# Position mix of a gated MLP block: both parts of the mixing weights in one 256-column matmul, and the later channel groups between the k tiles of the output projection

## The reference

```python
z = jax.nn.gelu(h @ w_in)
u, v = jnp.split(z, 2, axis=-1)
v = rmsnorm(v, v_g)
v = v.reshape(bsz, n, A_CHUNK, A_GROUPS, A_GDIM)           # chunks of 128 rows, 8 groups of 128 channels
ws = jnp.where(causal[None], w_s, jnp.zeros_like(w_s))      # 8 matrices of 128 x 128
s = jnp.einsum('gts,bnsgc->bntgc', ws, v) + b_s.T[None, None, :, :, None]
return (u * s.reshape(bsz, L, A_WIDTH)) @ w_out
```

## Time and profile before

| | |
|---|---|
| median of 3 runs | 1896.01 us (1891.55 to 1899.03) |
| the profiled execution's own time | 1891.51 us |
| its span, first to last instruction | 1889.7 us |
| TensorE busy | 1830.5 us, 97% of the span |
| VectorE busy | 1063.4 us, 56% |
| ScalarE busy | 769.9 us, 41% |
| GpSimd busy | 399.7 us, 21% |
| mean granted TensorE clock | 0.988 of full speed |

### The profile page before, as it was taken

The page is one execution under the profiler, slowest core; times in us unless marked ns, Lnnn a source line. Parts: engine busy times, 40 slices in busy tenths (PEclk is TensorE's granted clock), DMA queues, the critical chain, the costliest instruction groups (busy, mean ns, idle before and its releaser), DMA issues.

```text
span 1889.7 us, 20269 instructions
## 1 busy us (share of the span) xinstructions
PE 1830.5 (97%) x8329; PEld 1522.0 (81%) x8329; DVE 1063.4 (56%) x1025; ACT 769.9 (41%) x850; POOL 399.7 (21%) x386
## 2 busy tenths in 40 slices
PE   7999999999999999999979999998999999999997
PEld 5888888888888787888768888876888888888885
DVE  4463365265255665555575455657766666866664
ACT  5533543533433633344443434353333335333331
POOL 4442440450331033311112211132000002000001
PEclk9999999999999999999989999998999999999998
DMA  8545754753753778876957776799644545845542
GB/s 293 209 166 193 256 207 150 277 209 129 294 201 136 276 270 277 307 248 216 370 181 256 273 251 223 255 368 387 271 187 183 214 182 188 301 179 188 213 178 89
DMA packets 130268, 437.02 MB, mean 231 GB/s; under 512 B 7272, under 2 KB 8320, under 8 KB 115072
## 3 DMA queue, kind: packets, MB, share of 16 engines
q1 hardware_dynamic: 105920, 338.71, 50.0%
q0 software_dynamic: 23056, 88.61, 12.7%
q10 hardware_dynamic: 1200, 8.40, 1.1%
HBM read 309.87 MB, written 125.83 MB: 231 GB/s over the span
## 4 chain that ended last, share of the span: by engine, by line
PE 90%; DVE 3%; DMA 3%; ACT 1%; issue 1%; SPq 0%; DVEq 0%; POOL 0%; ACTq 0%
PE bank L1078 59%; PE bank L943 28%; PE bank L980 2%; DMA u_raw<-in_mlp_w 2%; PE bank L967 1%; DMA a_raw<-a2s 1%; DMA Y<-x1s 0%; DVE Y L894 0%; DVE sums L880 0%; DVE sums L887 0%; DVE r L877 0%; DVE u_lo L727 0%; DMA xin<-in_x 0%; DVE sums L885 0%; DVE sums L883 0%
## 5 line engine op out<-in xcount | busy, mean ns | idle before, releaser
L1078 PE MATMUL bank<-x_hi,u_hi 128*128 128x512 f32 x896 | 352.5, 393 | 21.5 <-DVE c L869 14.2
L1078 PE MATMUL bank<-d_hi,a_hi 128*128 128x512 f32 x896 | 350.0, 391 | 10.4 <-DVE Y L869 8.6
L1078 PE MATMUL bank<-x_lo,u_hi 128*128 128x512 f32 x896 | 351.0, 392 | 0.0
L1078 PE MATMUL bank<-x_hi,u_lo 128*128 128x512 f32 x896 | 350.8, 392 | 0.0
L1078 PE MATMUL bank<-d_lo,a_hi 128*128 128x512 f32 x896 | 349.6, 390 | 0.0
L1078 PE MATMUL bank<-d_hi,a_lo 128*128 128x512 f32 x896 | 349.5, 390 | 0.0
L727 DVE TENSOR_TENSOR u_lo<-u_raw,u_hi 128x1024 fp32r<-128x1024 f32 x112 | 144.4, 1290 | 232.8 <-ACT u_hi L516 232.7
L869 DVE TENSOR_TENSOR Y<-bank,Y 128x512 f32<-128x512 f32 x224 | 147.9, 687 | 196.0 <-PE bank L1078 191.4
L521 ACT ACTIVATE d_hi<-d_raw 128x2048 fp32r<-128x2048 f32 x56 | 107.4, 1918 | 318.0 <-DMA d_raw<-w2sum 188.2
L721 DVE TENSOR_TENSOR w_lo<-w_raw,w_hi 128x2048 fp32r<-128x2048 f32 x48 | 121.2, 2532 | 195.2 <-ACT w_hi L511 194.7
L1078 PEld LDWEIGHTS bank<-x_hi,u_hi 128*128 128x128 f32 x896 | 169.9, 190 | 59.3 <-issue 18.2
(11 more groups left out here) (105 smaller groups left out, 2819.0 us busy)
## 6 DMA issues: line engine op xcount, KB each, us to landing
a2s<-sums SPq DMA_DIRECT2D x32, 1792.0 KB, 12.6
a_raw<-a2s SPq DMA_DIRECT2D x56, 1024.0 KB, 7.1
w_raw<-in_a_w_in SPq DMA_DIRECT2D x32, 1024.0 KB, 6.5
job<-in_mlp_w POOLq DMA_DIRECT2D x32, 1024.0 KB, 6.8
u_raw<-w1sum SPq DMA_DIRECT2D x64, 512.0 KB, 4.2
d_raw<-w2sum SPq DMA_DIRECT2D x32, 1024.0 KB, 4.9
u_raw<-in_mlp_w SPq DMA_DIRECT2D x48, 512.0 KB, 5.6
d_raw<-in_mlp_w SPq DMA_DIRECT2D x24, 1024.0 KB, 5.1
```

Of the source, the lines that this page charges most:

```text
L1078: ins = pe.matmul(bank_of(g, j)[:, :], stationary[x_part][:, k, j * P:(j + 1) * P], moving[y_part][:, k, :], start=i in (0, 1, 3) and k == ...
```

## The change

The two parts of the mixing weights are put side by side in one tile, `wsT[:, g, HI or LO, :]`. A chunk of a group now takes two matmuls: the high part of v against both parts (256 columns, the product with the low part lands in the 128 columns beside the other), and the low part of v against the high part (128 columns, accumulated on the first 128). A group fills two banks instead of one (four chunks x 256 columns), so at most four groups fit: groups 0 and 1 in `BANK[0]`, even later groups in the first two banks of `BANK[1]`, odd ones in the last two. Groups 0 to 3 are mixed ahead of the output projection, groups 4 to 7 ahead of its k tiles 2 to 5, each once VectorE has read the group two before it (`mix_read`). `gate` adds the two halves: four operations of 256 columns where there was one of 512 (two on the first halves of the banks with gain and bias, two that add the second halves), then the product with `uT`. The transposes of the next block both go to `BANK[0]` and stand in the middle of units 10 and 11.

```diff
-    wsT = [sb(f"wsT_{n}", [P, G, P], F32R, R + (1 + i) * 4 * G * P) for i, n in enumerate(("hi", "lo"))]
+    wsT = sb("wsT", [P, G, 2, P], F32R, R + 4 * G * P)
...
+        def x_bank(q, half, j):
+            return BANK[1 - half if q == 0 else 0][j]
+
+        def mix_bank(g, t):
+
+            pair = g if g < 2 else 2 + g % 2
+            return BANK[pair // 2][2 * (pair % 2) + t // 2][:, t % 2 * 2 * P:(t % 2 + 1) * 2 * P]
...
             def gate(q, g):
                 dve.wait_ge(mix_done, q * G + g + 1)
-                dve.scalar_tensor_tensor(
-                    out=biased[:, g % 2, :].rearrange("p (n t) -> p n t", t=P),
-                    in0=BANK[g // 4][g % 4][:, :].rearrange("p (n t) -> p n t", t=P),
-                    scalar=g_v[:, g:g + 1], in1=bias_rows[:, g:g + 1, :].to_broadcast([P, TT, P]),
-                    op0=ALU.mult, op1=ALU.add).then_inc(mix_read, 1)
-                dve.wait_ge(mix_read, q * G + g + 1)
+                to = biased[:, g % 2, :].rearrange("p (n t) -> p n t", t=P)
+                pair = g if g < 2 else 2 + g % 2
+                banks = [BANK[pair // 2][2 * (pair % 2) + i][:, :].rearrange("p (n h t) -> p n h t", h=2, t=P)
+                         for i in range(2)]
+                for i in range(2):
+                    dve.scalar_tensor_tensor(
+                        out=to[:, 2 * i:2 * i + 2, :], in0=banks[i][:, :, 0, :], scalar=g_v[:, g:g + 1],
+                        in1=bias_rows[:, g:g + 1, :].to_broadcast([P, 2, P]), op0=ALU.mult, op1=ALU.add)\
+                        .then_inc(mix_biased, 1)
+                for i in range(2):
+                    dve.wait_ge(mix_biased, 2 * (q * G + g) + i + 1)
+                    dve.scalar_tensor_tensor(
+                        out=to[:, 2 * i:2 * i + 2, :], in0=banks[i][:, :, 1, :], scalar=g_v[:, g:g + 1],
+                        in1=to[:, 2 * i:2 * i + 2, :], op0=ALU.mult, op1=ALU.add).then_inc(mix_read, 1)
+                dve.wait_ge(mix_read, 2 * (q * G + g + 1))
...
-            def mix(q):
-                pe.wait_ge(v_ready, q * TT + TT)
-                pe.wait_ge(u_gelu, q * G + 4)
-                for g in range(G):
-                    if g >= 4:
-                        pe.wait_ge(u_gelu, q * G + g + 1)
-                    for t in range(TT):
-                        for n, (x_part, y_part) in enumerate(PASSES):
-                            ins = pe.matmul(BANK[g // 4][g % 4][:, t * P:(t + 1) * P],
-                                            vn[q % 2][x_part][:, t, g * P:(g + 1) * P],
-                                            wsT[y_part][:, g, :], start=n == 0, stop=n == 2)
-                    ins.then_inc(mix_done, 1)
+            def mix(q, g):
+
+                for t in range(TT):
+                    to = mix_bank(g, t)
+                    pe.matmul(to, vn[q % 2][HI][:, t, g * P:(g + 1) * P],
+                              wsT[:, g, :, :].rearrange("p h t -> p (h t)"), start=True, stop=False,
+                              skip_group_check=True)
+                    ins = pe.matmul(to[:, 0:P], vn[q % 2][LO][:, t, g * P:(g + 1) * P], wsT[:, g, HI, :],
+                                    start=False, stop=True, skip_group_check=True)
+                ins.then_inc(mix_done, 1)
...
-                mix(q)
-
-                pe.wait_ge(mix_read, q * G + 4)
+
+                def mixed(k):
+
+                    g = 4 + k - 2
+                    if 0 <= g - 4 < 4:
+                        pe.wait_ge(mix_read, 2 * (q * G + g - 1))
+                        mix(q, g)
+                    if k == 0:
+                        pe.wait_ge(mix_read, 2 * (q * G + 2))
+                    pe.wait_ge(y_ready, q * G + k + 1)
+
+                pe.wait_ge(v_ready, q * TT + TT)
+                pe.wait_ge(u_gelu, q * G + 4)
+                mix(q, 0)
+                mix(q, 1)
+                for g in range(2, 4):
+                    pe.wait_ge(u_gelu, q * G + 2 * g + 2)
+                    mix(q, g)
                 for a in range(2):
-                    if a == 1 and not last:
-                        xT_half(0)
-                    token_major(yT[q % 2], w + UO + a, 0, a,
-                                ready=lambda k: pe.wait_ge(y_ready, q * G + a * KU + k + 1))
-                pe.wait_ge(mix_read, q * G + 8)
-                if not last:
-                    pe.wait_ge(hT_ready, (q + 1) * KD + 4)
+                    token_major(yT[q % 2], w + UO + a, 0, a, ready=lambda k: mixed(a * KU + k))
+                pe.wait_ge(mix_read, 2 * (q * G + G))
                 for a in range(2):
                     token_major(yT[q % 2], w + UO + 2 + a, 1, a,
-                                between=(lambda: xT_half(1)) if a == 0 and not last else None)
+                                between=(lambda: xT_half(a)) if not last else None)
```

More of the change, by code:

```diff
@@ L188, in build @@
         v_hi_done, v_ready = sem("v_hi_done"), sem("v_ready")
-        mix_read, y_done = sem("mix_read"), sem("y_done")
+        mix_biased, mix_read, y_done = sem("mix_biased"), sem("mix_read"), sem("y_done")
         y_hi_done, y_ready = sem("y_hi_done"), sem("y_ready")
@@ L567, in split_h @@
                     act.wait_ge(xT_done, q * KD + k + 1)
-                    act.activation(hT[q % 2][HI][:, k, :], BANK[1 - half][j][:, :], ACT.Copy,
+                    act.activation(hT[q % 2][HI][:, k, :], x_bank(q, half, j)[:, :], ACT.Copy,
                                    scale=g_mix[:, k:k + 1]).then_inc(hT_hi_done, 1)
@@ L612, in block_act @@
                         split_w(w + 10)
-                if not last:
-                    split_h(q + 1, 0)
                 split_w(w + 11)
@@ L617, in block_act @@
                     split_w(w + 12)
+                    split_h(q + 1, 0)
+                    split_w(w + 13)
                     split_h(q + 1, 1)
-                    split_w(w + 13)
                 else:
@@ L640, in _ @@
                 act.wait_ge(ws_T, 4 * s + 4)
-                act.activation(wsT[HI][:, 4 * s:4 * s + 4, :], BANK[1][s][:, :], ACT.Copy)\
+                act.activation(wsT[:, 4 * s:4 * s + 4, HI, :],
+                               BANK[1][s][:, :].rearrange("p (g t) -> p g t", t=P), ACT.Copy)\
                     .then_inc(wsT_hi_done, 1)
@@ L750, in split_h @@
                     dve.wait_ge(hT_hi_done, q * KD + k + 1)
-                    dve.scalar_tensor_tensor(out=hT[q % 2][LO][:, k, :], in0=BANK[1 - half][j][:, :],
+                    dve.scalar_tensor_tensor(out=hT[q % 2][LO][:, k, :], in0=x_bank(q, half, j)[:, :],
                                              scalar=g_mix[:, k:k + 1], in1=f32(hT[q % 2][HI][:, k, :]),
@@ L841, in _ @@
                 dve.wait_ge(wsT_hi_done, s + 1)
-                dve.tensor_tensor(wsT[LO][:, 4 * s:4 * s + 4, :],
+                dve.tensor_tensor(wsT[:, 4 * s:4 * s + 4, LO, :],
                                   BANK[1][s][:, :].rearrange("p (g t) -> p g t", t=P),
-                                  f32(wsT[HI][:, 4 * s:4 * s + 4, :]), ALU.subtract).then_inc(wsT_done, 1)
+                                  f32(wsT[:, 4 * s:4 * s + 4, HI, :]), ALU.subtract).then_inc(wsT_done, 1)
             dve.wait_ge(bias_loaded, 16)
@@ L995, in xT_half @@
                 def xT_half(half):
[L996 to L1000, removed]
+                    pe.wait_ge(x1_attn, q * 2 * TT + TT)
+                    if half == 1:
+                        pe.wait_ge(hT_ready, (q + 1) * KD + 4)
+                    transposes(xin, half, 0, xT_done,
                                lambda t: pe.wait_ge(xn_ready, (q + 1) * TT + t + 1))
@@ L1017, in block_pe @@
                         feature_major(hT[q % 2], w + UU + 2 * half + a, half, a)
-                mix(q)
-                pe.wait_ge(mix_read, q * G + 4)
-                for a in range(2):
-                    if a == 1 and not last:
-                        xT_half(0)
-                    token_major(yT[q % 2], w + UO + a, 0, a,
-                                ready=lambda k: pe.wait_ge(y_ready, q * G + a * KU + k + 1))
-                pe.wait_ge(mix_read, q * G + 8)
-                if not last:
-                    pe.wait_ge(hT_ready, (q + 1) * KD + 4)
+                def mixed(k):
[13 more added lines that the diff above has]
+                    mix(q, g)
+                for a in range(2):
+                    token_major(yT[q % 2], w + UO + a, 0, a, ready=lambda k: mixed(a * KU + k))
+                pe.wait_ge(mix_read, 2 * (q * G + G))
                 for a in range(2):
                     token_major(yT[q % 2], w + UO + 2 + a, 1, a,
-                                between=(lambda: xT_half(1)) if a == 0 and not last else None)
+                                between=(lambda: xT_half(a)) if not last else None)
             pe.wait_ge(ident_done, 1)
```

## The result

The changed kernel takes 1906.0 us (median of 6 runs, 1903.7 to 1908.6) against 1895.4 of before in the same comparison: ratio 1.0057, 95% interval 1.0041 to 1.0073. It is slower by 10.7 us; the forecast was +12.

What follows compares the result with a forecast made beforehand. TensorE, 97% busy, bounds the kernel. Per block -3.3 + 2.8 + 1.5 + 1.1 + 0.5 = +2.7 us, with GpSimd's hits taken as +3.0, +12 in four: 1896 + 12 = 1908 us, range 1897 to 1917.

Steps and rivals of the forecast that it cites:

- The time: Whole kernel: 1908 us, from the median 1896 plus 12 in four blocks; chance of slower 0.63.
- rival 2: Output projection starves less, with no GpSimd hit and no lower clock: +1.3 us a block, 1901; chance 0.27.
- TensorE's part: Mix: a group takes 0.93 us instead of 1.34, so -3.3 us a block.
- rival 4: Mix: the 256-column matmul costs 0.224 us, nothing shortened, 1906 to 1914; 0.68 shared with the forecast and another rival.
- VectorE's part: Gate: 2.32 us against 1.39, +0.93 us a group; with `split_y` 2.93.
- The first wait: Ahead of k tile 0, TensorE waits for y 0: +2.8 us a block.
- The wait ahead of k tile 4: Output projection, after group 6 is mixed: TensorE waits for y 4, +1.1 us (0.9 to 1.1).
- the wait ahead of k tile 6: Output projection: y 6 comes 0.5 us after k 5 ends, +0.5 us a block.
- The lower clock: Matmuls behind the 2.8 us gap ahead of k tile 0 run at 1.2 instead of 2.4 GHz: +1.5 us.
- GpSimd's slowing: VectorE's uT and y of groups 2 to 4: two or three hits of 1.09 us, block's sum from +2.7 to +3.8.
- What costs nothing: Moved transposes (`xT_half`) and block 3's later SP load stay hidden; the second half's transposes have slack 2.3 us.
- Rival 3: VectorE's work stays hidden, no wait for y 0, TensorE keeps 3.3 us a block, 13 in all: 1883; chance 0.05.

Runs made afterwards that it cites:

- late_job: The changed kernel with GpSimd's job in the mix held until all y of the block are ready: 1906.7 us, ratio 1.0061 to before.
- long_gate: order_only with four operations of 256 columns a gate, two over each half of the one bank, mixed values doubled: 1903.4 us, ratio 1.0043 to before.
- one_op_gate: The changed kernel with one 512-column operation a gate over two banks, the high-v by low-weights product not added: 1895.2 us, ratio 0.9997 to before.
- late_split: The changed kernel with the split of unit 10's weights behind the last group instead of the fifth: 1902.3 us, ratio 1.0035 to before.
- fill: The changed kernel with group 3 mixed four times over, in the stretch where TensorE waited: 1903.7 us, ratio 1.0040 to before.
- order_only: The kernel of before, its mix and gate kept, in the change's new order of transposes and splits: 1895.2 us, ratio 0.9998 to before.
- hybrid3: Groups 0 to 2 as before, 3 to 7 two-bank with two operations a gate, five groups ahead of unit 8, late split: 1890.1 us, 0.9969 to before.
- two_op_gate: The changed kernel with two operations of 512 columns a gate over both banks, the same sum: 1906.0 us, ratio 1.0061 to before.

## Why the prediction was right, point by point

- **The time**: 1908 was forecast, 1906 measured, by the mechanism named. Block by block the excess is +3.2, +2.8, +2.2 and +3.1 us, against 3.0. That it is so close is in part luck. late_job has neither the lower clock nor a slowed operation, which is the case of rival 2: its blocks are +1.6 each against the +1.3 forecast for it. The clock and GpSimd together add 1.2 a block to that, not the 1.7 of the forecast (3.0 less 1.3). The waits were put too low by 0.3 a block, the clock and GpSimd too high by 0.5, and the two errors stand against each other.
- **TensorE's part**: -3.3 us a block. The pair takes 0.231 us, (114.97 - 111.73)/14, against 0.232 in the sum, so rival 4 (0.224 for the wide one alone) is out. Not in the sum was that the first matmul of 512 columns behind each piece of mix takes 0.29 us instead of 0.23, some 0.2 a block. The estimate by the Trainium skill (TensorE: Matmul & The Clock Gate, LDWEIGHTS) had 256 columns as free. The rows show no such split: the 256-column matmul is followed after 0.17 us, the 128-column one after 0.06. Only the pair can be compared, and that estimate's 0.224 is off by 0.007, 0.2 us a block.
- **VectorE's part**: +0.93 us a group; measured 2.30 a gate against 1.40, +0.90. The estimate by the Trainium skill (VectorE: DVE Perf Modes, TRN2 errata) of 0.91 agrees with that: by that rule one operation of 256 columns is 0.39 us, and they start 0.39 to 0.40 apart, though the record of one lasts 0.48.
- **The first wait**: 2.8 forecast, 2.76 to 2.77 measured in all four blocks. That it is the gate's length is shown from both sides: long_gate puts that gate behind the mix of before and loses, one_op_gate takes it out of the new one and wins the 10.7 us back.
- **The wait ahead of k tile 4**: 1.1 forecast, 0.93 to 1.21 measured; the wait ahead of k tile 6 0.5 and 0.36 (idle time starts where the last matmul's record ends, some 0.1 to 0.2 us late). late_split shows that the first of them is VectorE's queue.
- **The lower clock**: forecast in every block, found in three. The argument for it, that 2.8 us lies between two gaps that lowered the clock, doesn't carry: the change's own block 2 and late_job keep it after 2.77. Its 1.5 us is mis-stated as a term that adds: it delays k tile 1 by 1.3 to 1.6, but k tile 4 starts 22.8 to 23.1 us after the mix in those blocks and 22.2 in block 2, so 0.6 to 0.9 stays. The reason is the exchange with GpSimd: at the lower clock group 4 is mixed 1.3 to 1.5 us later and its product misses the job, and where the clock holds it is slowed by 0.6. fill takes the clock out and gets the slowing in its place.
- **GpSimd's slowing**: it hits one y in every block (1.78 to 1.79), which costs little by itself (the gate of group 4 starts 13.4 us after the mix both in block 2, which has it, and in late_job, which hasn't), and in block 2 the product of group 4 as well (1.33). That the four operations that read a bank aren't hit is borne out (0.88 for two of them at 427.70, inside the job). The forecast put the hits between 0 and +1.1 a block and took +0.3; block 2 against late_job says 0.6, from one execution each.
- **What costs nothing**: no wait at the transposes, at a block's start or at the start of the MLP; order_only is 0.9998 of before.
- **Rival 3** was given a gate of 0.94 us as the point at which it decides, from the wait for y 0 alone. That was incomplete: by the same working a gate of 1.39 us leaves a gain of 2.4 us a block, and one_op_gate, which has it, only gets back to before. The step missing was what VectorE waits for: it idles 1.2 to 1.5 us in three blocks of the change and 2.9 in one_op_gate for a group that TensorE holds back.

## What to carry to other kernels

A consumer that is slower than its producer is free only as long as the lead lasts: when a shortened producer stage feeds a chain that another engine must walk before TensorE can go on, price the time to the first and the time between results, not the sum of work. A form that saves TensorE time at a price in PSUM banks and VectorE time is best used for the groups behind the first few (hybrid3: -0.31% against +0.57% for all groups; the later split is part of that). Two costs can take turns: with one removed the other steps in, so remove both before calling either free. And work on another engine that slows VectorE is cheap only where VectorE has slack; moving it needs the same look at what then stands beside it.

## What the hardware showed that I had not expected

- An idle stretch of 2.65 to 2.77 us of TensorE cost the clock in 3 of 4 blocks of the change, 4 of 4 in late_split, 2 of 4 in two_op_gate and 0 of 4 in late_job, and one of 1.70 us cost it in block 2 of one_op_gate, while one of 1.80 in before and one of 2.86 in the MLP of the change left it whole: length alone doesn't decide it. In block 0 of the change the fall came at 118.9, 1 us after the matmuls had started again at 117.96; in block 1 at 269.1, ahead of the first matmul at 269.61. The row of the change's MLP, and the clock around it:

```profile
649.00 0.47 PE L1102 MATMUL bank<-x_hi,u_hi 128*128 128x512 f32 x1 [2.86 <-issue]
...
645.00:655.00 10.00, 7.14 (x34) 5.60 (x33) 6.68 (x5) 9.60 (x11) 0.00 (x0) 1.00 0.51 197
```

- A dependent VectorE operation on the same tile starts 0.86 us after a 512-column one that reads a bank in two_op_gate, where the record of the first ends after 0.75; the next one that depends on it 0.78.
